# Mixture of experts in a decoder step: the next expert's up products ahead of the down products, weight buffers as one ring in that order, rows gated ahead of the last scatter

## The reference, cut to what matters

```python
def expert(args):
    xe, e = args
    hu = xe @ w_up[e] + b_up[e]
    gate = jnp.minimum(hu[:, :D_FF], SWIGLU_LIMIT)
    lin = jnp.clip(hu[:, D_FF:], -SWIGLU_LIMIT, SWIGLU_LIMIT)
    glu = gate * jax.nn.sigmoid(SWIGLU_ALPHA * gate)
    return ((lin + 1.0) * glu) @ w_down[e] + b_down[e]
...
    x = x + gate_ffn * moe(h2)          # each token: its 4 experts' rows, weighted and summed
...
    final RMSNorm over x
```

## Time and profile before

| | us |
|---|---|
| median of 3 runs (1352.71 to 1359.05) | 1354.84 |
| profiled execution | 1354.65 |
| its span, first to last instruction | 1352.8 |
| TensorE busy | 1219.4 (90%) |
| VectorE busy | 390.5 (29%) |
| ScalarE busy | 221.8 (16%) |
| moved by DMA | 465.61 MB, mean 344 GB/s |

### The profile page before, as it was taken

How to read it: one execution, slowest core, us unless ns; L and a number is a source line. 1 busy time by engine, 2 the same in 40 slices (tenths; PEclk the granted TensorE clock), 3 DMA queues, 4 the chain that set the end, 5 groups by cost and what they waited for, 6 DMA issues and landing times.

```text
span 1352.8 us, 23254 instructions
## 1 busy us (share of the span) xinstructions
PE 1219.4 (90%) x8796; PEld 563.0 (42%) x8797; DVE 390.5 (29%) x850; ACT 221.8 (16%) x369; POOL 72.6 (5%) x148
## 2 busy tenths in 40 slices
PE   5999999979699999998899998899877998997895
PEld 4655457634433344442244443344222343342342
DVE  0173214653722122321122222212212232221126
ACT  3012242001301111111110111111111111111111
POOL 1010011450000000000000000000000000000002
PEclk9999999888899999998899998899988998998998
DMA  9836234673368999999999999999999999999992
GB/s 368 341 130 253 99 120 187 172 243 137 126 250 344 422 422 414 423 422 422 422 422 422 373 423 422 422 421 391 422 422 422 422 422 422 422 421 422 422 422 109
DMA packets 79956, 465.61 MB, mean 344 GB/s; under 512 B 8594, under 2 KB 26326, under 8 KB 27826
## 3 DMA queue, kind: packets, MB, share of 16 engines
q1 hardware_dynamic: 76898, 458.86, 83.4%
q10 hardware_dynamic: 2640, 5.68, 1.3%
q0 software_dynamic: 384, 0.59, 0.1%
HBM read 458.35 MB, written 6.16 MB: 343 GB/s over the span
## 4 chain that ended last, share of the span: by engine, by line
PE 61%; DMA 20%; SPq 10%; DVE 3%; issue 3%; POOL 2%; ACT 1%; POOLq 0%; DVEq 0%; ACTq 0%
DMA mem<-in_w_up 19%; PE psum L968 16%; PE psum L1004 11%; SPq L405 10%; PE psum L1014 8%; PE psum L624 6%; PE psum L939 4%; PE psum L605 3%; PE psum L811 2%; PE psum L461 2%; PE psum L628 2%; PE psum L732 1%; DMA mem<-in_mod_chunks 1%; PE psum L749 1%; PE psum L1036 1%
## 5 line engine op out<-in xcount | busy, mean ns | idle before, releaser
L968 PE MATMUL psum<-mem 128*32 128x512 f32 (+2 forms) x2432 | 415.6, 641 | 77.9 <-DMA mem<-in_w_up 66.9
L968 PEld LDWEIGHTS psum<-mem 128*32 128x32 f32 (+2 forms) x2432 | 115.1, 124 | 370.1 <-issue 202.6
L1004 PE MATMUL psum<-mem 128*32 128x512 f32 (+3 forms) x1024 | 213.7, 594 | 0.0
L1974 DVE TENSOR_SCALAR mem<-psum 128x256 f32<-128x256 f32 (+3 forms) x32 | 19.2, 601 | 592.6 <-PE psum L972 592.6
L1014 PE MATMUL psum<-mem 128*128 128x512 f32 (+1 forms) x396 | 156.9, 607 | 3.6 <-issue 1.9
L1993 DVE TENSOR_TENSOR mem<-mem,psum 128x1024 f32<-128x1024 f32 (+1 forms) x96 | 100.3, 1045 | 100.1 <-PE psum L1014 100.1
L1004 PEld LDWEIGHTS psum<-mem 128*32 128x32 f32 (+3 forms) x1024 | 81.3, 127 | 105.2 <-issue 96.4
L939 PEld LDWEIGHTS psum<-mem 128*128 128x128 bf16 x2304 | 79.3, 99 | 18.9 <-issue 18.6
L1339 ACT ACTIVATE mem<-mem 128x256 f32<-128x256 f32 (+3 forms) x32 | 17.9, 559 | 422.3 <-DVE mem L1974 422.3
L624 PE MATMUL psum<-mem 128*128 128x512 f32 x192 | 84.2, 595 | 0.0
L939 PE MATMUL psum<-mem 128*128 128x64 bf16 (+1 forms) x2304 | 83.2, 197 | 0.0
(11 more groups left out here) (262 smaller groups left out, 839.5 us busy)
## 6 DMA issues: line engine op xcount, KB each, us to landing
mem<-in_w_up SPq DMA_DIRECT2D x256, 1024.0 KB, 25.2
mem<-in_w_down SPq DMA_DIRECT2D x128, 1024.0 KB, 18.3
mem<-in_mod_chunks SPq DMA_DIRECT2D x12, 2048.0 KB, 12.1
mem<-in_in_chunks SPq DMA_DIRECT2D x8, 2048.0 KB, 8.8
mem<-in_out_chunks SPq DMA_DIRECT2D x2, 2048.0 KB, 10.2
mem<-in_x_prompt ACTq DMA_DIRECT2D x2, 1024.0 KB, 7.4
mem<-in_state_ret SPq DMA_DIRECT2D x4, 512.0 KB, 6.7
mem<-in_state_mlstm_c SPq DMA_DIRECT2D x4, 512.0 KB, 9.0
```

Of the source, the lines that this page charges most:

```text
L968: last = pe.matmul(out, xg[:, c, cols], moving, start=(c == 0), stop=False)
L1004: last[c] = pe.matmul(psum[slots * q:slots * q + slots, 6 + u, :], turned, piece_slot(UP + c, 2, D)[:, piece % 2, 512 * u:512 * u + 512], ...
```

## The change

- **Order on TensorE.** An iteration is now: up(e), gather(e+1), scatter of tiles 0 and 1, **down(e-1)**, turn of the activations of e, turn of the weights of e-1, scatter of tile 2. Expert 0 has a form of its own without scatter and down (`first_expert`), and down(31) comes behind the loop (`last_down`). What is scattered in iteration e is the result of down(e-2).
- **Buffers.** The twelve buffers are refilled in the new order of use: up(e) pieces 0 to 3 in buffers 8 to 11, 4 to 7 in buffers 0 to 3, down(e-1) in buffers 4 to 7. Ahead of the loop all of up(0) and the first half of up(1) are loaded. down(31) goes to buffers 8 to 11.
- **Waits on TensorE.** `xg_ready` moves into `up`; `G_ready` and `added` ahead of it are asked for only for experts of more than 64 slots, and never by expert 0 of the first round. `gather` waits for `actT_ready` of the expert before, the turn of the activations (now into banks 4 and 5) for the third `added`.
- **DVE** makes the weighted one-hot of expert e-1 and adds the rows scattered in its iteration. **POOL** picks two bias columns per expert (`bsel` and `bsel_down`).
- **End.** Tile order is 2, 0, 1. The result of down(31) is copied out in halves, each half multiplied by `gateF_p` ahead of the scatter (`yd_gated`), so that tiles 0 and 1 come out of the scatter gated and need only the addition. Tile 2, the samples, is scattered ungated first. SP issues three output stores, one per tile.

```diff
+        def up_slot(c, first):
+            return c if first else (UP + c) % PIECES
+        def down_slot(c, last):
+            return UP + c if last else DOWN + c
...
+            def load_ahead(e, it):
+                for c in range(4):
+                    sp.wait_ge(piece_done[up_slot(c, False)], it - 1)
+                    load_up(e, c, False)
+            def load_rest(e, it):
+                for c in range(4, UP):
+                    sp.wait_ge(piece_done[up_slot(c, False)], it)
+                    load_up(e, c, False)
+                for c in range(DOWN):
+                    sp.wait_ge(piece_done[down_slot(c, False)], it)
+                    load_down(e - 1, c, False)
...
+                for s in (2 * c, 2 * c + 1):
+                    if s < UP:
+                        load_up(0, s, True)
+                    else:
+                        load_up(1, s - UP, False)
+            load_rest(1, 1)
+            with sp.Fori(2, NE) as e:
+                load_ahead(e, e)
+                load_rest(e, e)
+            load_end(NE - 1)
...
+            def up(ig, it, slots, first):
+                pe.wait_ge(S("xg_ready"), ig + 1)
+                if slots > 64 and not isinstance(it, int):
+                    pe.wait_ge(S("G_ready"), it + 1 if first else it)
+                    pe.wait_ge(S("added"), 3 * it + 1 if first else 3 * it - 2)
...
+            def first_expert(ig, it, count, count_next):
+                by_size(pe, count, lambda slots: up(ig, it, slots, True))
+                gather(ig + 1, count_next, None if isinstance(it, int) else it)
+                if not isinstance(it, int):
+                    pe.wait_ge(S("y_copied"), it + 1)
+                by_size(pe, count, lambda slots: turn_activations(it, slots, True))
+
+            def expert(r, e, it, count, count_before, count_next):
                 ig = r * (NE + 1) + e
-                pe.wait_ge(S("xg_ready"), ig + 1)
-                pe.wait_ge(S("G_ready"), it + 1)
-                pe.wait_ge(S("added"), 3 * it + 1)
-                by_size(pe, count, lambda slots: up(it, slots))
-                gather(ig + 1, count_next)
-
-                pe.wait_ge(S("y_copied"), it + 1)
+                n = it - 1
+                by_size(pe, count, lambda slots: up(ig, it, slots, False))
+                gather(ig + 1, count_next, it)
+
+                pe.wait_ge(S("G_ready"), n + 1)
+                pe.wait_ge(S("y_copied"), n + 1)
+                pe.wait_ge(S("added"), 3 * n + 1)
                 pe.wait_ge(S("gate_ready"), it + 1)
                 pe.wait_ge(S("lin_clipped"), it + 1)
-                scatter(it, 0)
+                scatter(n, 0)
                 pe.wait_ge(S("xg_ready"), ig + 2)
-                scatter(it, 1)
-                by_size(pe, count, lambda slots: turn_activations(it, slots))
...
+                scatter(n, 1)
+                by_size(pe, count_before, lambda slots: down(n, slots, False))
+                pe.wait_ge(S("added"), 3 * n + 3)
+                by_size(pe, count, lambda slots: turn_activations(it, slots, False))
+                turn_weights(n)
+                scatter(n, 2)
+
+            def last_down(n, count):
+                pe.wait_ge(S("G_ready"), n + 1)
+                pe.wait_ge(S("y_copied"), n + 1)
+                pe.wait_ge(S("added"), 3 * n + 1)
+                scatter(n, 0)
+                pe.wait_ge(S("actT_ready"), n + 1)
+                scatter(n, 1)
+                turn_weights(n)
+                scatter(n, 2)
+                by_size(pe, count, lambda slots: down(n, slots, True))
 
             def last_scatter(its):
                 pe.wait_ge(S("G_ready"), its + 1)
-                pe.wait_ge(S("y_copied"), its + 1)
                 pe.wait_ge(S("added"), 3 * its + 1)
...
+                for u in range(2):
+                    pe.wait_ge(S("y_copied"), its + 1 + u)
+                    last = pe.matmul(psum[64 * u:64 * u + 64, 0, :], G[:, tok(2)], yd[:, u, :], start=True, stop=True)
+                last.then_inc(S("last_scattered"), 1)
+                pe.wait_ge(S("y_gated"), 2)
+                for t in range(2):
+                    for u in range(2):
+                        last = pe.matmul(psum[:, 2 + 2 * t + u, :], G[:, tok(t)], yd_gated[:, u, :], start=True, stop=True)
+                    last.then_inc(S("last_scattered"), 1)
...
+            def expert(r, e, it, count, count_before):
+                one_hot(r, e + 1, r * (NE + 1) + e + 1)
+                weights(r, e - 1, count_before)
+                by_size(dve, count, lambda slots: swiglu(it, slots))
+                add_scattered(it - 1)
...
+                TT(yd_gated[:, 1, :], psum[:, 7, :], gateF_p[:, 512:D], ALU.mult).then_inc(S("y_gated"), 1)
+                dve.wait_ge(S("y_copied"), its + 1)
+                TT(yd_gated[:, 0, :], yd[:, 0, :], gateF_p[:, 0:512], ALU.mult).then_inc(S("y_gated"), 1)
+                dve.wait_ge(S("last_scattered"), 1)
...
+                for t in range(2):
+                    dve.wait_ge(S("last_scattered"), 2 + t)
+                    TT(x2[:, t, :], x2[:, t, :], flat(2 + 2 * t, D), ALU.add).then_inc(S("x3_ready"), 1)
```

More of the change, by code:

```diff
@@ L263, in S @@
             return sems[name]
-        loaded = [S(f"slot{c}_loaded") for c in range(6)]
-        used = [S(f"slot{c}_used") for c in range(6)]
+        loaded = [S(f"slot{c}_loaded") for c in range(4)]
+        used = [S(f"slot{c}_used") for c in range(4)]
         UP, DOWN = 8, 4
@@ L316, in build @@
         NCH = len(CH)
-        USES = [len(range(c, NCH, 4)) if c < 4 else 0 for c in range(6)]
+        USES = [len(range(c, NCH, 4)) for c in range(4)]
         def chunk_source(name):
@@ L395, in _, with load_up, load_down, load_end @@
                 load_state(i)
[L397 to L405, removed]
+            def load_up(e, c, first):
+                s = up_slot(c, first)
+                sp.dma_start(piece_slot(s, 2 * D), a["w_up"][0][e, 128 * c:128 * c + 128, :]).then_inc(piece_in[s], 16)
+            def load_down(e, c, last):
+                s = down_slot(c, last)
+                src = a["w_down"][0][e, 256 * c:256 * c + 256, :].rearrange("(p h) n -> p h n", h=2)
+                sp.dma_start(piece_slot(s, 2, D), src).then_inc(piece_in[s], 16)
+            def load_ahead(e, it):
[9 more added lines that the diff above has]
+                    load_down(e - 1, c, False)
+            def load_end(uses):
+                for c in range(DOWN):
+                    sp.wait_ge(piece_done[down_slot(c, True)], uses)
+                    load_down(NE - 1, c, True)
             for i in range(2 * H):
@@ L1056, in _, with count_at @@
-            most = pe.value_load(counts_i[0:1, NE:NE + 1], min_val=0, max_val=NTOK)
+            def count_at(e):
+                where = slice(e, e + 1) if isinstance(e, int) else bass.ds(e, 1)
+                return pe.value_load(counts_i[0:1, where], min_val=0, max_val=NTOK)
+            first_expert(0, 0, count_at(0), count_at(1))
+            with pe.Fori(1, NE) as e:
+                expert(0, e, e, count_at(e), count_at(e - 1), count_at(e + 1))
+            last_down(NE - 1, count_at(NE - 1))
@@ L1057, in _ @@
+            most = pe.value_load(counts_i[0:1, NE + 1:NE + 2], min_val=0, max_val=NTOK)
             with pe.If(most > BIG_BLOCK):
                 with pe.Fori(1, ROUNDS) as r:
-                    gather(r * (NE + 1), None)
-                    with pe.Fori(0, NE) as e:
-                        expert(r, e, r * NE + e, None, None)
+                    pe.wait_ge(S("actT_ready"), r * NE)
+                    pe.wait_ge(S("added"), 3 * r * NE + 1)
+                    gather(r * (NE + 1), None, None)
+                    first_expert(r * (NE + 1), r * NE, None, None)
+                    with pe.Fori(1, NE) as e:
+                        expert(r, e, r * NE + e, None, None, None)
+                    last_down(r * NE + NE - 1, None)
@@ L1370, in _, with count_at @@
             act.wait_ge(S("counts_ready"), 1)
[L1371 to L1375 removed]
+            def count_at(e):
+                where = slice(e, e + 1) if isinstance(e, int) else bass.ds(e, 1)
+                return act.value_load(counts_i[0:1, where], min_val=0, max_val=NTOK)
@@ new lines, in weighted @@
+            def weighted(r, e, slots):
+                first = r * 128 if isinstance(r, int) else None
+                sl = K("slots")[:, bass.ds(r * 128, 128)] if first is None else K("slots")[:, first:first + slots]
+                for t in range(NT):
+                    n = ROWS[t]
+                    last = TSC(Pg[0:n, t, :].rearrange("p (q s) -> p q s", s=slots),
+                               sl[0:n, :].unsqueeze(1).to_broadcast([n, 128 // slots, slots]),
+                               pos[0:n, t, bass.ds(e, 1)], gate[0:n, t, bass.ds(e, 1)], ALU.is_equal, ALU.mult)
+                last.then_inc(S("Pg_ready"), 1)
```

327 lines of the change are left out of this document (173 added, 154 removed).

## The result

The change made the kernel slower, by little: 1358.39 us median (1355.27 to 1362.09, 20 runs) against 1355.0 us for the kernel before (20 runs), ratio 1.0033, 95% interval 1.0018 to 1.0049 (the ratio is taken over all these runs; it is not that of the two medians). 1338.6 was predicted. The profiled execution took 1356.41 us, its span 1354.2.

The account below looks back on a forecast made before the run. The expert stage was taken as bound by back-to-back weight DMA, with 7% slack on TensorE. The terms -6.0 - 9.4 - 4.4 + 3.7 = -16.1 us against 1354.65 gave 1338.6 us, range 1332 to 1348.

Parts of the forecast that it names:

- Part 1: Start of expert 0: no wait for `added`, full clock, earlier first refill; -6.0 us, bounds 0 and -6.0.
- Nothing but the copy stands ahead: Start of up(0): only ACT's copy of the gathered tile is left to wait for; start near 366.0 instead of 369.31.
- Rival A: Start of expert 0 gains nothing (another wait replaces `added`, or clock is 1.2 GHz); 1342 to 1348 us, chance 0.10.
- Part 2: First DMA gap, behind up(0): 6.9 us of idle time in place of 16.3, -9.4 us; bounds -10.5 and -5.
- down(0) with its slow pieces is hidden behind that queue: After the first gap: up(1) and up(2) free pieces three times as fast as DMA fills them, covering down(0).
- no run here shows a refill by itself: First gap: instruction refill cost unseen beside one 1.88 us gap; one or two such gaps more, inside the bound.
- Part 3: Later DMA gaps, as behind experts 11 and 17: 2.0 us idle in place of 6.4, -4.4 us; bounds -5.4 and 0.
- Part 4: New waits in the expert stage: all moved beside other work, costed at nothing; shortest cover an up, 7.05 us.
- Rival C: Expert stage: a new wait isn't covered and TensorE's chain per expert becomes the bound; 1363 us, chance 0.05.
- Part 5: Tail from last landing to end: longer order ahead of down(31), T + 33, +3.7 us; bounds +1.5 and +6.
- The sum: Whole kernel: -6.0 - 9.4 - 4.4 + 3.7 = -16.1 us against 1354.65, so 1338.6 us; forecast with bounds 0.70.
- The likeliest rivals: Start gains nothing, 1344 us, chance 0.10; or rates after 420 stay and tail grows to its bound, 1345, chance 0.10.

Follow-up runs that it names:

- before_early: Kernel before, with `added` given ahead of the zeroing of acc, so that up(0) need not wait for it; ratio to before 0.9989 [0.9973, 1.0005].
- one_form: Changed kernel, with TensorE's program of expert 0 cut to the one form it takes (96 slots, gather of 64); ratio to before 0.9972 [0.9953, 0.9992].
- before_peeled: Kernel before, with expert 0 taken out of TensorE's loop as its own copy of the code; ratio to before 1.0104 [1.0076, 1.0131].
- hold_refills: Changed kernel, with SP holding down(0)'s four refills back until expert 1's gather is over; one execution, 1363.66 us.
- old_tail: Changed kernel with the end of the kernel before (whole copy, tiles 0, 1, 2, gates behind the scatter, two stores); ratio to before 1.0037 [1.0020, 1.0054].

## Why the prediction was wrong

**Part 1 (-6.0 predicted, -1.8 measured).** "Nothing but the copy stands ahead" failed. The earlier trace rows show the 4.73 us as a wait for the zeroing, and I took it as the whole price; a second cause without a semaphore, code to be fetched, ended at nearly the same time (before_early). Up(0) now starts 3.1 us after the copy and 0.6 of 3.3 us is gained; the clock is 0.57 in 366 to 368, and SP's first issue comes 4.4 us after the start, not 2.9. The working was right for a kernel without that fetch: one_form measured -6.3, with the clock at 1.00 as that step took it. Rival A (a start that gains nothing, "another wait takes the place") had this mechanism and a chance of 0.10, but its price, 1342 to 1348, held nothing for what came behind the start.

On the clock the Trainium skill (TensorE: Matmul & The Clock Gate, "What's actually happening") says that throttled is the default and activity releases it. Both sides can be seen here: up(0) went on at 1.00 over its first 5 us behind 1.15 us of idle time (one_form), and was at 0.57 behind 4.12 us (the changed kernel).

**Part 2 (-9.4 predicted, about +10 measured).** This is the step that decided. I allowed 0.9 us for a fetch in the DMA's gap (6.0 in place of 5.1), where the one row there was has 1.88 us, and held two for the bound; at nothing I put what the new code costs in expert 1. The change makes a second copy of up, gather and turning, and there were five gaps behind up(0), 17.5 us. Of these 1.7 are the DVE wait that I had counted (one_form shows it as such); the lower clock adds 1.5 on up(0), 1.3 on up(1), 1.8 on the gather and 2.4 on the scatter. 15.8 + 7.0 = 22.8 us, close to the 22 by which down(0) starts later (62.7 instead of 41). So "down(0) with its slow pieces is hidden behind that queue" no longer held: the queue covered 19.9 us. The wording "no run here shows a refill by itself" was a warning that I didn't price: what the traces of before could not show was exactly what the change adds.

The Trainium skill (Advanced Engine Details and Errata, "ISA Cache") gives lines of 16 KB, 256 instructions, and only a few of them per engine. The packets agree (0.41 MB in 25). The section gives no duration for a refill. By its line size, the added code could have been counted in lines ahead of the run. The packets say what really came in: six more in the changed kernel, fifteen more in before_peeled.

**Part 3 (-4.4 predicted, -4.3 measured).** Right: 421 GB/s from 450 on, 2.1 us of idle time, no dip after experts 11 and 17.

**Part 4 (0 predicted).** Right. Waits of TensorE from 365 to 1340 in the changed kernel:

```profile
PE psum L1019 <- DMA mem<-in_w_up: 53.8, 56, 1.4
...
PE psum L1019 <- DVE mem L2127: 2.6, 3, 0.9
PE psum L1057 <- DMA mem<-in_w_down: 2.3, 4, 1.0
...
PE psum L1067 <- ACT mem L1463: 1.5, 1, 1.5
```

What is left of slack is 53.8 us against 66.9, and waits on other engines come to a few us in the whole stage. Rival C was priced for these and didn't happen.

**Part 5 (+3.7 predicted, +2.0 measured).** Inside its bounds. The tail of the changed kernel, with the last landing at 1322.6:

```profile
1328.26 7.03 PE L1057 MATMUL psum<-mem 128*64 128x512 f32 x31
...
1336.36 1.23 DVE L2139 TENSOR_TENSOR mem<-mem 128x1024 f32<-128x1024 f32 x1
...
1338.98 1.07 PE L1124 MATMUL psum<-mem 128*64 128x512 f32 x2 [1.75 <-ACT mem L1475]
...
1347.91 1.17 POOL L1530 TENSOR_SCALAR mem<-mem 128x1 f32<-128x1 f32 x1 [1.27 <-ACT mem L1506]
...
1349.74 1.29 DVE L2200 SCALAR_TENSOR_TENSOR mem<-mem 128x1024 f32<-128x1024 f32 x1 [0.72 <-POOL mem L1531]
```

Down(31) ends at T + 12.7 (T + 11.8 foreseen), DVE's preparation behind it at T + 15.0 (T + 14.8), so DVE is late as said. From there the end came in 16.6 us, not 18.2. The terms that I listed for that stretch add up to 15.2 to 16.3 us, so about 2 us of the +3.7 stand in no term. POOL's last pair took 1.17 + 0.55 us here, the low end of my 1.8 to 2.9. Other executions of the same end took up to 33.2 us (one_form).

**The sum.** -1.8 + 9.8 - 4.3 + 2.0 = +5.7 us where -16.1 was forecast: 19 of the 22 us of error are part 2, 4 are part 1, the tail gives 2 back. The likeliest rivals were all about waits and rates that the trace of before shows; none priced the code itself. Two slips moved nothing: the DMA row is at 9 from slice 13 to slice 38, not 12 to 39, and the low bound of part 2, with no fetch and no spacing, comes to -11.2 by its own terms, not -10.5.

## What to carry to other kernels

Before a loop gets a peeled first iteration or a second body, count the code that is added and where it runs for the first time: here the single gaps took 0.7 to 6.0 us of TensorE, in sum more while weights stream, and twelve buffers of lead didn't absorb them. An idle time with one named releaser is an upper bound of what the removal brings; look for whatever else ends at the same moment, above all in places that run once. The reordering of this DMA bound loop paid when one body served all iterations: the same order and ring gave +0.3% with two bodies and -0.5 to -0.6% with one (and another preload).

## What the runs showed of the hardware that was not expected

- Copying a loop body of TensorE, with nothing else changed, cost 1.0% (1.0104 [1.0076, 1.0131]): 15 packets of 16 KB, five gaps of 1.4 to 4.0 us, and a DMA that idled 18.5 us longer.
- The gaps at the same three places took 5.4 us beside 33 GB/s of weights (hold_refills, one trace) and 12.5 and 12.0 us beside 398 and 392 (the changed kernel and old_tail).
- The break inside a gather moved from behind 14 products to behind 60 when code ahead of it was taken out (the changed kernel and one_form).
- The gap at up(0)'s start is 3 to 4 us after the copy with hardly any weight traffic (3.7, 3.8, 3.1 us), and 0.1 us with one form in place of four. Branches, register loads and the other forms went together there, so which of them costs the 3 us wasn't taken apart.
- In the kernel before, expert 1 takes forms of 32 slots that no expert had taken, and no gap over 0.8 us appears. So it seems to be the first passage over a region of code that costs, not the first execution of each instruction. This was not tested by itself, and the fifth gap of before_peeled doesn't fit it.
- ScalarE loads its table once for line 1426 where the kernel before did so 32 times (41.1 us in sum, line 1339). No run tests what that alone does to the time.
